# Attention scores of a hybrid decoder layer: one 384-column product for both heads' low key parts, keys loaded per unit, and full-height operands for the sample's new rows

## The reference, cut to what matters

```python
q = rope(rms_norm(q.reshape(B, T, N_HEADS, HEAD_DIM), q_norm_g), pos)      # 16 heads of 64
k = rope(rms_norm(k.reshape(B, T, N_KV_HEADS, HEAD_DIM), k_norm_g), pos)   # 4 key heads
...
def sw_attention_core(q, k, v, qpos, kpos, sinks):
    s = jnp.einsum('bnqkgd,bnskd->bnkgqs', q, k) * (HEAD_DIM ** -0.5)
    rel = qpos[:, :, None] - kpos[:, None, :]
    mask = (rel >= 0) & (rel <= WINDOW) & (kpos[:, None, :] >= 0)          # WINDOW = 128
    s = jnp.where(mask[None, :, None, None], s, -jnp.inf)
    m = jnp.maximum(jnp.max(s, axis=-1, keepdims=True), sink)
    e = jnp.exp(s - m)
    pr = e / (jnp.sum(e, axis=-1, keepdims=True) + jnp.exp(sink - m))
    return jnp.einsum('bnkgqs,bnskd->bnqkgd', pr, v)
```

## Time and profile before

| | us |
|---|---|
| median of 3 runs | 1165.45 |
| lowest, highest | 1164.78, 1166.21 |
| the profiled execution | 1165.09 |
| its span, from first to last instruction | 1163.3 |
| TensorE busy in it | 1156.3 (99%) |
| VectorE, ScalarE, GpSimd busy | 563.9, 395.9, 407.7 |
| granted TensorE clock, mean | 0.999 of full |

### The profile page before, as it was taken

The page is one execution under the profiler, slowest core; times in us unless marked ns, Lnnn a source line. Parts: engine busy times, 40 slices in busy tenths (PEclk is TensorE's granted clock), DMA queues, the critical chain, the costliest instruction groups (busy, mean ns, idle before and its releaser), DMA issues.

```text
span 1163.3 us, 20002 instructions
## 1 busy us (share of the span) xinstructions
PE 1156.3 (99%) x7656; PEld 1143.1 (98%) x7656; DVE 563.9 (48%) x1045; ACT 395.9 (34%) x954; POOL 407.7 (35%) x191
## 2 busy tenths in 40 slices
PE   8999999999999999999999999999999999999998
PEld 8999999999999999999999999999999999999998
DVE  5566774112556566564726465832363451163322
ACT  6433334233766767666110010321321030031112
POOL 4433332333212222223333344335432532374310
PEclk9999999999999999999999999999999999999999
DMA  9425466313455555652611111072223232412211
GB/s 303 168 73 149 141 165 181 94 46 87 132 154 158 153 154 134 166 148 74 218 54 51 37 50 36 23 276 76 92 75 124 82 124 77 135 65 64 65 38 56
DMA packets 145791, 130.83 MB, mean 112 GB/s; under 512 B 49039, under 2 KB 134439, under 8 KB 145727
## 3 DMA queue, kind: packets, MB, share of 16 engines
q1 hardware_dynamic: 131063, 106.21, 30.0%
q10 hardware_dynamic: 14664, 23.74, 7.1%
HBM read 94.82 MB, written 37.12 MB: 113 GB/s over the span
## 4 chain that ended last, share of the span: by engine, by line
PE 99%; DMA 1%; SPq 0%; DVE 0%; issue 0%; DVEq 0%
PE ps L684 75%; PE ps L822 11%; PE ps L933 2%; PE ps L708 2%; PE ps L1092 1%; PE ps L964 1%; PE ps L947 1%; PE ps L784 1%; PE ps L698 1%; PE ps L968 1%; PE ps L951 1%; PE ps L1061 1%; DMA xr<-in_x_prompt 1%; PE ps L888 0%; PE ps L868 0%; PE ps L1040 0%
## 5 line engine op out<-in xcount | busy, mean ns | idle before, releaser
L684 PE MATMUL ps<-m_hi,w_hi 128*128 128x352 f32 x1704 | 556.1, 327 | 0.1
L684 PE MATMUL ps<-m_lo,w_hi 128*128 128x352 f32 x1704 | 548.1, 322 | 0.0
L684 PE MATMUL ps<-m_hi,w_lo 128*128 128x352 f32 x1704 | 369.8, 325 | 0.0
L684 PEld LDWEIGHTS ps<-m_hi,w_hi 128*128 128x128 f32 x1704 | 320.9, 188 | 1.3 <-issue 0.5
L684 PEld LDWEIGHTS ps<-m_lo,w_hi 128*128 128x128 f32 x1704 | 320.7, 188 | 0.0
L597 POOL TENSOR_TENSOR w_hi<-raw_a,w_one 128x1024 fp32r<-128x1024 f32 x41 | 78.9, 1923 | 683.4 <-PE ps L684 371.4
L684 PEld LDWEIGHTS ps<-m_hi,w_lo 128*128 128x128 f32 x1704 | 289.8, 188 | 0.0
L599 POOL TENSOR_TENSOR w_lo<-raw_b,w_hi 128x1024 fp32r<-128x1024 f32 x41 | 111.1, 2709 | 3.2
L599 POOL TENSOR_TENSOR w_lo<-raw_a,w_hi 128x1024 fp32r<-128x1024 f32 x41 | 104.1, 2539 | 3.2
L822 PE MATMUL ps<-w_lo,m_hi 128*128 128x256 f32 (+1 forms) x360 | 99.4, 282 | 0.0
L822 PE MATMUL ps<-w_hi,m_hi 128*128 128x256 f32 x320 | 92.3, 288 | 0.0
(11 more groups left out here) (248 smaller groups left out, 1429.9 us busy)
## 6 DMA issues: line engine op xcount, KB each, us to landing
raw_a<-in_w_in SPq DMA_DIRECT2D x25, 512.0 KB, 3.7
raw_b<-in_w_in SPq DMA_DIRECT2D x25, 512.0 KB, 4.6
qk_d<-qkst ACTq DMA_DIRECT2D x20, 512.0 KB, 5.6
gate_d<-gst ACTq DMA_DIRECT2D x16, 528.0 KB, 3.4
gin<-gate_d SPq DMA_DIRECT2D x16, 528.0 KB, 3.6
qt<-qk_d SPq DMA_DIRECT2D x64, 128.0 KB, 3.5
kt<-qk_d SPq DMA_DIRECT2D x96, 64.0 KB, 2.5
vt<-v_d SPq DMA_DIRECT2D x84, 64.0 KB, 2.2
```

Source lines behind the costliest of these rows:

```text
L684: last = nc.tensor.matmul(ps[:, 3 * parity + c, 0:CH], w, x[:, k, CH * c:CH * c + CH], start=(k == 0 and w is wh and x is src_hi), stop=(k ...
```

## The change

- Scores: instead of four products of 192 columns, one of 2 x 192 and two of 192. For the first, the stationary operand is a new tile `q_high`: the high parts of the first pair of heads on partitions 0 to 63 and those of the second pair on 64 to 127. The moving operand is two planes of `kt`: the keys' low parts on partitions 0 to 63 above zeros, and zeros above the same low parts on 64 to 127. So it leaves low x low out. The other two are as before, queries' both parts against the keys' high parts.
- VectorE fills `q_high` with two copies per unit (`stack_high`), one unit ahead: after the low parts of the probabilities and before the reciprocals. TensorE's first scores of a unit wait for the second copy (`q_high_put`). For unit 0 the copies stand at the end of the sample's last group, before `scale_za`.
- `kt` is double-buffered by unit and holds three planes of 256 keys; SP loads both blocks for every unit, in two transfers, and the first of them wait until `kt` is cleared (now 1536 numbers per partition, before 1024).
- VectorE's loop over the units ends one turn earlier, and the last eight units are written out.
- Sample: the products with the new rows use all 128 partitions, where the rest are zeros: `q_sum` of the key heads gets zeros in place of a second copy, and ScalarE clears the rest of `v_group` and `spt` in each group (four instructions).

```diff
@@ def load_q_k
-                for slot in ((2, 0) if m < 4 else (1,)):
-                    for half in range(2):
-                        sp.dma_start(kt[HD * half:HD * half + HD, kv, :, slot, :].bitcast(F32),
-                                     qk_d[NH + kv, :, tok].rearrange("(s e) n -> e s n", s=2))\
-                            .then_inc(unit_loaded[kv], 16)
+                first = isinstance(t, int) and t == 0
+                seen = slice(0, P) if first else bass.ds(t * P - P, 2 * P)
+                for half in range(2):
+                    dst = kt[HD * half:HD * half + HD, m % 2, 0:2 + half:1 + half, P if first else 0:2 * P]
+                    sp.dma_start(dst.bitcast(F32), qk_d[NH + kv, :, seen].rearrange("(s e) n -> e s n", s=2))\
+                        .then_inc(unit_loaded[kv], 16)
@@ def scores
                 if s == 0:
-                    pe.wait_ge(unit_loaded[kv], i * 160 + (96 if m < 4 else 160))
+                    pe.wait_ge(unit_loaded[kv], t * 64 + 64)
+                    pe.wait_ge(q_high_put, u + 1)
                 bank = round_of("S", u, s, m, first)
-                k0 = (P if m < 4 else 0) + HD * s
+                seen = slice(HD * s, HD * s + KW)
+                nc.tensor.matmul(ps[:, bank, :].rearrange("p (b n) -> p b n", b=2)[:, :, 0:KW],
+                                 q_high[:, slot, s, :, :].rearrange("p g n -> p (g n)"), kt[:, slot, 1:3, seen],
+                                 start=True, stop=False)
                 for b in range(2):
-                    for part in range(2):
-                        keys = kt[:, kv, part, :, :].rearrange("p s n -> p (s n)")[:, k0:k0 + KW]
-                        last = nc.tensor.matmul(ps[:, bank, 256 * b:256 * b + KW],
-                                                qt[:, slot, s, 2 * b:2 * b + 2, :].rearrange("p g n -> p (g n)"), keys,
-                                                start=(part == 0), stop=(part == 1))
+                    last = nc.tensor.matmul(ps[:, bank, 256 * b:256 * b + KW],
+                                            qt[:, slot, s, 2 * b:2 * b + 2, :].rearrange("p g n -> p (g n)"),
+                                            kt[:, slot, 0, seen], start=False, stop=(b == 1))
@@ VectorE
+            def stack_high(m, t):
+
+                dve.wait_ge(unit_loaded[m % 4], t * 64 + 64)
+                for b in range(2):
+                    last = v.tensor_copy(q_high[HD * b:HD * b + HD, m % 2, :, :, :],
+                                         qt[0:HD, m % 2, :, 2 * b:2 * b + 2, :].bitcast(F32))
+                last.then_inc(q_high_put, 1)
...
-                    v.memset(kt[:, :, :, 1, :].bitcast(F32), 0.0).then_inc(zero_done, 1)
+                    v.memset(kt[:].bitcast(F32), 0.0).then_inc(zero_done, 1)
...
                 step.did(v.memset(sst[:, 0:1], 0.0))
+                if last_group:
+                    stack_high(0, 0)
                 scale_za(kv, 1)
...
                     split_probs(u - 1, (m - 1) % 8)
+                if not (isinstance(i, int) and u == PBLK * NKV - 1):
+                    stack_high((m + 1) % 8, i * 2 + (m + 1) // 4)
                 reciprocals(u, m)
@@ TensorE, sample
-                nc.tensor.matmul(ps[:, 7, P:SK], q_sum[0:HD, P * v:P * v + P], k_new[0:HD, NS * v:NS * v + NS],
+                nc.tensor.matmul(ps[:, 7, P:SK], q_sum[:, P * v:P * v + P], k_new[:, NS * v:NS * v + NS],
...
-                nc.tensor.matmul(ps[:, 7, 0:P], v_group[0:NS].rearrange("p s e -> p (s e)"), spt[0:NS, 1, :],
+                nc.tensor.matmul(ps[:, 7, 0:P], v_group[:].rearrange("p s e -> p (s e)"), spt[:, 1, :],
@@ ScalarE, sample
+                    for rest in (slice(NS, HD), slice(HD, P)):
+                        a.memzero(v_group[rest])
+                        a.memzero(spt[rest, 1, :])
```

More of the change, by code:

```diff
@@ L260, in build @@
             gst = sb("gst", [P, 2, T], scope=s3)
-            kt = sb("kt", [P, NKV, 2, 3, P], F32R, scope=s3)
+            kt = sb("kt", [P, 2, 3, 2 * P], F32R, scope=s3)
+            k_gap = sb("k_gap", [P, 1024], scope=s3)
             qt = sb("qt", [P, 2, 2, G, HD], F32R, scope=s3)
+            q_high = sb("q_high", [P, 2, 2, 2, HD], F32R, scope=s3)
             msk = sb("msk", [P, 2, 2, KW], scope=s3)
@@ L330, in build @@
         att_done, att_read = sem("att_done"), sem("att_read")
-        low_copied, low_added = sem("low_copied"), sem("low_added")
+        low_copied, low_added, q_high_put = sem("low_copied"), sem("low_added"), sem("q_high_put")
         masks_loaded, zero_done = sem("masks_loaded"), sem("zero_done")
@@ L462, in load_q_k @@
             def load_q_k(u, t, m):
-                tok, kv = bass.ds(t * P, P), m % 4
+                kv = m % 4
                 for a in range(2):
@@ L503, in _ @@
                 sp.wait_ge(qk_stored[h], 16 * 10)
+            sp.wait_ge(zero_done, 1)
             for m in range(2):
@@ L919, in round_of, with scores @@
                 return 6 + (att_bank(kind, m, first) + s) % 2
-            def scores(u, m, i, s, first=False):
+            def scores(u, m, t, s, first=False):
                 slot, kv = m % 2, m % 4
@@ L975, in attention_half @@
                 after, between = {k0: [], k0 + 1: [], k0 + 2: [], k0 + 3: []}, {}
-                after[k0].append(lambda: scores(u, m, i, 0, first and m == 0))
-                after[k0 + 1].append(lambda: scores(u, m, i, 1, first and m == 0))
+                after[k0].append(lambda: scores(u, m, t, 0, first and m == 0))
+                after[k0 + 1].append(lambda: scores(u, m, t, 1, first and m == 0))
                 if not first or m >= 1:
@@ L1387, in _ @@
                 attention_half(0, m, first=True)
-            with dve.Fori(1, PBLK // 2) as i:
+            with dve.Fori(1, PBLK // 2 - 1) as i:
                 for m in range(8):
                     attention_half(i, m)
+            for m in range(8):
+                attention_half(PBLK // 2 - 1, m)
             end, last_tok = PBLK * NKV, slice(SEQ - P, SEQ)
@@ L1679, in take_back @@
                         col = NS * (q_head(j) + h)
-                        for half in range(2):
+                        for half in range(2 if j >= 2 else 1):
                             a.activation(q_sum[HD * half:HD * half + HD, col:col + NS],
                                          ps[HD * h:HD * h + HD, bank, 0:NS], ACT.Copy)
+                        if j < 2:
+                            a.memzero(q_sum[HD:P, col:col + NS])
                 a.activation(qkst[:, j % 2, 0, c0:c0 + w], ps[:, bank, 0:w], ACT.Copy).then_inc(back_hi, 1)
```

## The result

| | before | after |
|---|---|---|
| median, us | 1165.12 (4 runs) | 1183.0 (4 runs) |
| lowest, highest | 1164.67, 1166.21 | 1182.06, 1185.08 |
| the profiled execution | 1165.09 | 1183.5 |
| its span | 1163.3 | 1181.7 |
| granted TensorE clock, mean | 0.999 | 0.994 |

The changed kernel is slower: its ratio to the kernel before is 1.0155, 95% interval 1.0137 to 1.0172. The forecast was 1181.4 us.

A forecast was written before the change was run, and what follows sets the result against it. TensorE was taken to bound the kernel: 1165.1 - 2.9 (scores) - 1.9 (sample) + 16.2 (six stops) + 0.4 (unit 27's copies) + 4.1 (first unit) = 1181.0, against the median 1181.4 us. Own range 1178 to 1185; with rivals 1164 to 1185.

The forecast's parts named there:

- What bounds: Whole kernel: TensorE is 99% of the chain, so time is the distances between matmul starts plus any new TensorE wait.
- Scores, 2.9 less: TensorE's score products: each set falls from 0.44 to 0.395 us, 64 sets, 2.9 us saved, bounds 2.6 to 3.2.
- Sample, 1.9 less: Sample's small products at full height: 0.28 us saved on values, 0.18 on scores, in each of four groups, 1.9 us.
- Clearings, loads of the keys, longer VectorE loop: nothing: ScalarE's four extra clearings per group and first keys loaded about half a microsecond later: both cost nothing.
- The copies exclude POOL, and both lose, 2.7 six times: VectorE's copies in units 3, 7, ...: each waits for a POOL instruction, delaying TensorE 2.7 us, six times, 16.2 us.
- Unit 28: Copies made in unit 27: the first wins, the second waits for POOL's L597 alone, costing 0.4 us.
- First unit, 4.1: Unit 0's copies: both wait for POOL, the second ending at 290.5; TensorE starts at 290.7 instead of 286.59, 4.1 us.
- The clock: TensorE's clock dropping after a stop as long as the first unit's: only in the range's upper end, not the sum.
- the first rival: First copy beats POOL everywhere: 0.4 us in seven units, 2.4 in the first, total 1165.9, no change; chance 0.20.
- First copy wins everywhere: Same as the first rival: the second copy alone waits for POOL, total 1165.9 us; chance 0.20.
- No meeting: Rival: copies run at the slow rate, 0.43 each, beside POOL; only the first unit costs 0.6, total 1161.3; chance 0.15.

The follow-up runs named there:

- experiment 5: Experiment 1's kernel with unit 0's pair of copies moved behind the last sample group's reciprocal and unit 1's ahead of the sample's gate; 1158.16 us, ratio 0.9945.
- experiment 6: The kernel before with only the sample's full-height operands and ScalarE's clearings added; 1161.69 us, ratio 0.9975.
- experiment 1: The changed kernel with the two copies to `q_high` written as a reduction over an axis of length one, same place and moment; 1160.13 us, ratio 0.9956.
- experiment 3: The changed kernel with a tiny POOL instruction ahead of each weight chunk's first rounding, so POOL starts a little later; 1165.98 us in one run.
- experiment 4: The changed kernel with one copy instead of two, the second pair of heads left without its low x high part; 1161.13 us in one run.
- experiment 2: The changed kernel without VectorE's copies, SP loading `q_high` from DRAM in four more transfers per unit; 1170.6 us, ratio 1.0049.

## Why the prediction was right, and where it was not, point by point

- **What bounds.** Right as far as it went: TensorE's distances and one new wait, with the clock behind that wait, which the sum left out, account for the spans to 0.2 us.
- **Scores, 2.9 less.** The term was small by 0.4: 3.35 in experiment 5, 0.052 a set instead of 0.045, above the bound of 3.2. The price of a 192-column product was read as 0.11; the four of before took 0.112 each and the set of after 0.396.
- **The Trainium skill, "TensorE: Matmul & The Clock Gate".** Measured is a set that is shorter by 0.05 with the same 768 columns, in 64 places. The formula that the prediction took from the section Back-to-back issue gap would have given about nothing; but the section gives it for a single isolated product and says itself that it is too low at few columns, so it was no second rule for this place. The section LDWEIGHTS (107 ns a load) agrees with the distances of 0.103 to 0.112.
- **Sample, 1.9 less.** The step that failed is the price of ten full-height products. It was taken from the eight that stood between others of less height, 0.114 each; ten in a row cost 0.103. So each group saves 0.68 instead of 0.46, in all 2.7 (2.9 by experiment 6). Entering the run costs too: in the earlier trace rows the first small product starts at 257.20, 0.10 after its turn; in the kernel after it starts at once.
- **Clearings, loads of the keys, longer VectorE loop: nothing.** Right as far as the balance can tell: it closes to 0.2 us without them.
- **The copies exclude POOL, and both lose, 2.7 six times.** Right in place, order and mechanism, by the rows of unit 4 and by experiments 1, 3 and 4. The six stops are 15.4 instead of 16.2, as two of them were 2.3 to 2.4. The call that mattered was that 0.04 us behind POOL is lost. It is: the first copy started 0.05 behind POOL in the six units and lost each time.
- **Unit 28 (its copies are made in unit 27, by which the prediction names it), 0.4.** Right: 0.46.
- **First unit, 4.1.** The step that failed is the moment of the first copy, put at 286.17, 0.05 behind POOL's 286.12. The copies before it began 0.60 ahead of POOL's instruction in the kernel before and 0.98 ahead in the one after (282.31 and 283.29), since the values' products save 0.39 and not 0.28, and the small clearing didn't hold the copy up: it starts at 283.14, beside the clearing. So it won by 0.15, and the stop was 2.30. The second copy waited as forecast for such a win (2.4, under the first rival).
- **The clock.** The step left out of the sum. The prediction had a drop only in the range's upper end, for the first stop; four stops had one, 6.4 us. The start of TensorE after a stop was left out too: 0.11 in each of the four stops where it can be told apart, 0.4 us. Nothing of before could show that, as TensorE has no stop there in this stretch.
- **The total.** On the profiled executions the forecast was 15.9 us more, and the spans differ by 18.4. Step by step: scores -0.4, sample -0.8, six stops -0.8, first unit -1.8, unit 28 +0.1, clock +6.4, products right behind the other stops +0.4, the start of this execution -0.35, unassigned -0.2: 2.5 in all. Against the medians it is 1.6 (1181.4 and 1183.0). The forecast came this near because 3.8 us that it had too much stand against 6.8 that it had not; the mechanism doesn't owe anything to that.
- **The rivals.** "First copy wins everywhere" happened in units 0 and 28 alone, and where experiment 3 forced it, the seven stops had the price forecast for them; the total agreed by luck. "No meeting" was excluded by the 0.28 of the undisturbed copies, and made real by experiment 1: 1160.1 for 1161.3, as scores and sample save 1.3 more and the stop of unit 1 (1.23) was not foreseen.
- **The Trainium skill, "SBUF — State Buffer", section SBUF: two separate sides.** In the rows, a copy of 0.29 waits for the whole of a POOL instruction that started 0.05 before, and a TENSOR_REDUCE of 0.41 at the same place runs through. The page's rule, by which a copy excludes POOL when it is in the two-port mode, fits the first; no run here shows in which mode a copy is. It doesn't say how two waiting copies and POOL's next instruction come after each other: here POOL's next one began between them in all six units.

## What to carry to other kernels

Before a small copy is put on VectorE into idle time, look at what POOL does in that stretch: the price of a fast SBUF-to-SBUF copy is not its 0.3 us but the whole of the POOL instruction that began before it, and a pair of copies can pay for two of them. A form that doesn't exclude POOL is worth its 0.12 us more (22.9 us here), and if only one fast instruction stands there, the idle time may hold it. And when a change makes TensorE stop for some microseconds, count the clock behind the stop as a term of its own.

## What the runs showed of the hardware that was not expected

- Of nine stops of 2.3 to 2.7 us (seven in the kernel after, one each in experiments 2 and 3), six had 3.4 us at the half clock with them, and three had none; the length of the stop does not tell them apart (2.68 in unit 4 with a drop, 2.70 in unit 12 without). The stops of 0.14 to 0.6 in experiment 3 had none either. In the kernel after the clock fell between 0.5 us before TensorE started again and 1.4 behind it. What decides stays open. The runs of the kernel after vary with it: 1182.06 us at a mean granted clock of 0.996, 1185.08 at 0.992.
- Whether the first copy or POOL's 128x1024 instruction wins turns between two starts that lie 0.07 us apart in the kernel after: recorded 0.05 behind POOL the copy lost in six of six units, recorded 0.016 ahead of POOL it won. Between these two that kernel has no case.
- VectorE's tensor-by-tensor product with both operands in SBUF took 2.50 in experiment 1, beside a POOL instruction that had started 0.19 before, so it isn't only copies that wait. In experiment 5 it started 0.01 ahead of POOL's instruction and took its 0.43; POOL's then took 2.67 instead of 2.40.
- Ten full-height small products in a row stand 0.103 apart, eight between others of less height 0.114.
